# Modulation matrix-vector products of a transformer kernel: from TensorE to VectorE, GpSimd and ScalarE

## What is computed

```python
s_c = jax.nn.silu(c)
s_cc = jax.nn.silu(c_ctx)
for i in range(DEPTH):                                  # 2 layers
    mx = jnp.split((s_c @ ada_w[i] + ada_b[i])[:, None, :], N_MOD, axis=-1)
    mc = jnp.split((s_cc @ ada_w[i] + ada_b[i])[None, None, :], N_MOD, axis=-1)
    x = ffn_step(x, norm_g[i, 0], mx[0], mx[1], mx[2], ffn_w_in[i, 0], ffn_w_out[i, 0])
    xc = ffn_step(xc, norm_g[i, 0], mc[0], mc[1], mc[2], ffn_w_in[i, 0], ffn_w_out[i, 0])
...
def ffn_step(s, g, shift, scale, gate, w_in, w_out):
    return s + 0.5 * gate * swiglu(modulate(rms_norm(s, g), shift, scale), w_in, w_out)
```

## Time and profile before

| What | Value |
|---|---|
| median of 3 runs | 3329.41 us (3328.68 to 3330.70) |
| profiled execution: span from the first to the last instruction | 3327.2 us |
| PE busy, share of the span | 3144.5 us, 95% |
| DVE busy | 1994.1 us, 60% |
| ACT busy | 1111.8 us, 33% |
| POOL busy | 34.6 us, 1% |
| mean granted TensorE clock | 0.976 |

### The profile page before, as it was taken

How to read it: one execution, slowest core, us unless ns; L and a number is a source line. 1 busy time by engine, 2 the same in 40 slices (tenths; PEclk the granted TensorE clock), 3 DMA queues, 4 the chain that set the end, 5 groups by cost and what they waited for, 6 DMA issues and landing times.

```text
span 3327.2 us, 48292 instructions
## 1 busy us (share of the span) xinstructions
PE 3144.5 (95%) x19226; PEld 2638.7 (79%) x19226; DVE 1994.1 (60%) x2728; ACT 1111.8 (33%) x1124; POOL 34.6 (1%) x34
## 2 busy tenths in 40 slices
PE   6999997999999999998899899989989989998898
PEld 4777774777777888785699899847869979985798
DVE  6566567566665454546566666745656666664466
ACT  5333333333333222322343434321014334342333
POOL 0000002000000000000000000000000000000000
PEclk9999998999999999999999999989999999998999
DMA  7344440344441322131144354410014554432154
GB/s 307 128 165 163 174 152 13 139 151 164 164 165 63 113 76 108 69 132 46 39 173 179 124 189 176 145 38 1 1 43 164 189 171 163 178 139 45 64 189 164
DMA packets 59429, 421.56 MB, mean 127 GB/s; under 512 B 6600, under 2 KB 7752, under 8 KB 9392
## 3 DMA queue, kind: packets, MB, share of 16 engines
q1 hardware_dynamic: 57056, 407.33, 33.1%
q0 software_dynamic: 2288, 13.01, 1.7%
HBM read 419.24 MB, written 1.07 MB: 126 GB/s over the span
## 4 chain that ended last, share of the span: by engine, by line
PE 87%; DVE 8%; ACT 2%; issue 2%; DMA 1%; DVEq 0%; SPq 0%; ACTq 0%
PE ps_o L1466 9%; PE ps_o L1467 9%; PE ps_o L1468 9%; PE ps_g L1466 7%; PE ps_u L1467 7%; PE ps_g L1467 7%; PE ps_u L1466 7%; PE ps_u L1468 7%; PE ps_g L1468 7%; PE ps_g L1481 2%; PE ps_o L1473 2%; PE ps_o L1604 2%; PE ps_o L1605 2%; DVE wlo L840 2%; PE ps_o L1667 1%
## 5 line engine op out<-in xcount | busy, mean ns | idle before, releaser
L840 DVE TENSOR_TENSOR wlo<-wraw,whi 128x2048 fp32r<-128x2048 f32 x386 | 877.5, 2288 | 354.1 <-ACT whi L562 353.3
L562 ACT ACTIVATE whi<-wraw 128x2048 fp32r<-128x2048 f32 x386 | 733.3, 1911 | 1041.1 <-PE ps_u L1468 420.4
L1466 PE MATMUL ps_o<-ah,wlo 128*128 128x256 f32 (+1 forms) x1408 | 468.5, 333 | 15.2 <-issue 13.6
L1466 PE MATMUL ps_g<-hh,wlo 128*128 128x256 f32 (+1 forms) x1408 | 459.0, 326 | 17.7 <-DVE hl L865 12.2
L1467 PE MATMUL ps_o<-al,whi 128*128 128x256 f32 (+1 forms) x1408 | 459.1, 326 | 0.0
L1467 PE MATMUL ps_u<-hl,whi 128*128 128x256 f32 (+1 forms) x1408 | 458.6, 326 | 0.0
L1467 PE MATMUL ps_g<-hl,whi 128*128 128x256 f32 (+1 forms) x1408 | 458.2, 325 | 0.0
L1468 PE MATMUL ps_o<-ah,whi 128*128 128x256 f32 (+1 forms) x1408 | 457.5, 325 | 0.0
L1468 PE MATMUL ps_u<-hh,whi 128*128 128x256 f32 (+1 forms) x1408 | 456.9, 325 | 0.0
L1466 PE MATMUL ps_u<-hh,wlo 128*128 128x256 f32 (+1 forms) x1408 | 456.9, 325 | 0.0
L1468 PE MATMUL ps_g<-hh,whi 128*128 128x256 f32 (+1 forms) x1408 | 456.8, 324 | 0.0
(11 more groups left out here) (366 smaller groups left out, 3977.6 us busy)
## 6 DMA issues: line engine op xcount, KB each, us to landing
wraw<-in_W SPq DMA_DIRECT2D x387, 1024.0 KB, 4.8
scr<-bias_rows POOLq DMA_DIRECT2D x8, 384.0 KB, 8.1
x<-in_XT POOLq DMA_DIRECT2D x1, 2048.0 KB, 10.8
scr<-in_ICNT POOLq DMA_DIRECT2D x1, 2048.0 KB, 9.7
x<-in_MEMT POOLq DMA_DIRECT2D x2, 1024.0 KB, 7.8
cst<-in_CST POOLq DMA_DIRECT2D x1, 1799.5 KB, 15.1
out<-x SPq DMA_DIRECT2D x1, 1024.0 KB, 4.8
scr<-in_LORA POOLq DMA_DIRECT2D x1, 384.0 KB, 3.4
```

Of the source, the lines that this page charges most:

```text
L562: nc.scalar.activation(whi[:, n % SLOTS, :], wraw[:, n % SLOTS, :], ACT.Copy).then_inc(w_hi, 1)
L840: tt_(wlo[:, n % SLOTS, :], wraw[:, n % SLOTS, :], whi[:, n % SLOTS, :].bitcast(f32), sub).then_inc(w_lo, 1)
L1466: mm(out, a[1], b[0], start=first, stop=False)
```

## The change

ada_w no longer goes through `W` and PE. It is stored transposed as `ADA`, 144 blocks of 128 output features by 1024 (0.5 MB each). c and c_ctx come spread over all partitions (`CB`, 1 MB). For each block b, DVE multiplies it by silu(c) and sums along the row in one instruction (`ada_sum` on DVE); POOL multiplies it by silu(c_ctx) (`ada_products`) into one of two buffers, and ACT sums that one with an accumulating copy (`ada_sum` on ACT). Blocks lie in six slots of their own: SP issues the first 16 (shift and scale of FFN 0), POOL the rest, each after its slot has been read by both. 24 blocks come before the loop of FFN 0 (8 gate blocks of them between the norm and the loop), six in each of the 20 passes. The first norm goes tile by tile: tile d waits for the sums of blocks 2d and 2d + 1 only. `ada_turn`, the zeroing of rows and the 72 chunks of ada in the stream are gone. The table `icnt` of the pooling stage is a quarter of its size, and the constants of 1.8 MB (`cst` from `cos` on) are loaded after the last block, since the DVE sums write their unused product there.

```diff
-STREAM = [("ada", 0, [1] * ADA_FIRST), ("ffn", 0, FFN_ADA_TILES), ("pool", 0, [8]), ("ffn", 1, FFN_ADA_TILES),
+STREAM = [("ffn", 0, FFN_TILES), ("pool", 0, [8]), ("ffn", 1, FFN_TILES),
...
+            sp.dma_start(ada_c, CB).then_inc(cb_in, 16)
             sp.dma_start(vec[:], VEC).then_inc(c_in, 16)
-            for s in range(SLOTS):
+            for b in range(ADA_SLOTS):
+                block(b)
+            sp.dma_start(cst[:, 0:cat["cos"]], CST[:, 0:cat["cos"]]).then_inc(c_in, 16)
+            for s in range(2):
                 sp.dma_start(wraw[:, s, :], W[s * 128:(s + 1) * 128, :]).then_inc(w_here[s], 16)
...
+            for b in range(ADA_SLOTS, ADA_SCALE):
+                sp.wait_ge(ad_prod, b - ADA_SLOTS + 1)
+                sp.wait_ge(ad_dve, b - ADA_SLOTS + 1)
+                block(b)
...
+                for b in range(first, last):
+                    ada_landed(pool, b)
+                    if b >= 2:
+                        pool.wait_ge(ad_acc, b - 1)
+                    nc.gpsimd.tensor_tensor(ada_p[:, b % 2, :], ada_w[:, b % ADA_SLOTS, :], ada_c[:, 1, :], mult).then_inc(ad_prod, 1)
+                    if ADA_SCALE <= b + ADA_SLOTS < end:
+                        pool.wait_ge(ad_prod, b + 1)
+                        pool.wait_ge(ad_dve, b + 1)
+                        block(b + ADA_SLOTS)
...
+            def ada_sum(b, i=None):
+
+                act.wait_ge(ad_prod, b + 1 if i is None else i * ADA_PER_PASS + (b + 1))
+                p = ada_p[:, b % 2, :]
+                nc.scalar.activation(p, p, ACT.Copy, accum_out=mod_col(b, 1, i)).then_inc(ad_acc, 1)
...
                 for d in range(KT):
+                    if part == 0:
+                        if d == 2:
+                            split_hi(0)
+                            split_hi(1)
+                        if d:
+                            ada_sum(2 * d)
+                            ada_sum(2 * d + 1)
+                        act.wait_ge(ad_col, d + 1)
...
+                if f == 0:
+                    for b in range(ADA_SCALE, ADA_GATE):
+                        ada_sum(b)
                 silu(DONE[n0], g0 or None)
...
                     split_hi(n0 + 5, i, step, per)
+                    ada_sums(0, 2, i)
                     silu(i * step + DONE[n0 + 2], i + (g0 + 1))
+                    ada_sums(2, 4, i)
                     for n in range(n0 + 6, n0 + 5 + per):
                         if n - SLOTS == n_down:
+                            ada_sums(4, 6, i)
                             act.wait_ge(mm_done, i * step + DONE[n_down])
...
+                    if ada is not None:
+                        for b in range(ada, ada + ADA_PER_PASS):
+                            ada_sum(b, i)
+                    product(i + (g0 + 1), i * step + DONE[n_up])
+                    down(n_down, i * step + DONE[n_down - 1])
+                    hidden(i + (g0 + 1))
+                    split_lo(n_up + SLOTS, i, per)
+                    split_lo(n_down + SLOTS, i, per)
...
+            def ada_sum(b, i=None):
+
+                slot = b % ADA_SLOTS
+                ada_landed(dve, b, i)
+                if b >= 2:
+                    dve.wait_ge(ad_dve, b - 1 if i is None else i * ADA_PER_PASS + (b - 1))
+                stt(ada_junk[:, b % 2, :], ada_w[:, slot, :], 1.0, ada_c[:, 0, :], mult, mult, accum_out=mod_col(b, 0, i)).then_inc(ad_dve, 1)
```

More of the change, by code:

```diff
@@ L198, in pack @@
     for kind, i, _ in STREAM:
[L199 to L202, removed]
+        if kind == "ffn":
+            chunks += ffn_order(*(f1 + f2)[i])
         elif kind == "pool":
@@ L247, in ffn_pass @@
     def ffn_pass(f):
-        tiles = FFN_ADA_PASS if f < 2 else FFN_PASS
         n0 = FIRST["ffn", f]
[L251 to L254, removed]
+        n = len(FFN_PASS)
+        return n, sum(max(t, 1) for t in FFN_PASS), sum(FFN_PASS), n0 + 3, n0 + 4, n0 + 2 + n * (GROUPS - 1)
     with ExitStack() as ctx:
@@ L623, in hidden, with ada_sums @@
                     nc.scalar.activation(ah[:, :, 0:N], tmp[:, :, 0:N], ACT.Copy).then_inc(a_hi, 1)
-                per, step, _, _, n_down, _, n_last = ffn_pass(f)
+                per, step, _, _, n_down, n_last = ffn_pass(f)
+                ada = ADA_GATE + f * ADA_LOOP if f < 2 else None
+                def ada_sums(first, last, i):
+                    if ada is not None:
+                        for b in range(ada + first, ada + last):
+                            ada_sum(b, i)
+                if f == 0:
+                    for b in range(ADA_SCALE, ADA_GATE):
+                        ada_sum(b)
                 silu(DONE[n0], g0 or None)
@@ L908, in hidden, with down @@
                     tt_(al[:, :, 0:N], tmp[:, :, 0:N], ah[:, :, 0:N].bitcast(f32), sub).then_inc(a_ready, 1)
-                def down(n, done, between=lambda d: None):
+                def down(n, done):
                     for d in range(KT):
@@ L913, in down @@
                         residual(ps_o[:, (TILE0[n] + d) % BANKS, :], d, N, gate)
-                        between(d)
+                if f == 0:
+                    for b in range(ADA_SCALE, ADA_GATE):
+                        ada_sum(b)
+                    ada_gate()
                 product(g0, DONE[n0 + 1], g0 > 0)
@@ L1484, in sum_squares, with norm @@
                 st["sums"] = max(st["sums"], end)
-            def norm(N, split=True, part=None, again=False):
+            def norm(N, split=True, again=False):
                 if again:
@@ L1490, in norm @@
                 sum_squares(N, KT)
-                if part is not None:
-                    ada_turn(part)
-                keep_clock(N // 64 - 1 if part is None else 3, BANK[3])
+                keep_clock(N // 64 - 1, BANK[3])
                 st["k"], st["sums"] = st["k"] + 1, 0
@@ L1685, in y_split @@
                 pe.wait_ge(y_ready, st["y"])
-            pe.wait_ge(ad_lo, 1)
-            for n in range(ADA_FIRST):
-                ada(n)
-                sum_squares(NTOK, min(n - 2, KT))
-            norm(NTOK, part=0)
+            pe.wait_ge(c_in, 32)
+            norm(NTOK)
             ffn(0, NTOK)
-            norm(NTOK, False, part=1)
+            norm(NTOK, False)
             n = FIRST["pool", 0]
@@ L1706, in _ @@
             ffn(1, NTOK)
-            norm(NTOK, part=2)
+            norm(NTOK)
             ffn(2, NTOK)
```

242 lines of the change are left out of this document (109 added, 133 removed), and 1 row of the table sizes.

## The result

The changed kernel takes **3409.6 us** (median of 4 runs, 3406.9 to 3411.2) against 3329.1 us before on the same chip: **ratio 1.0237, 95% interval 1.0225 to 1.025**. It is slower by 80 us; 3388 was forecast, inside a range of 3285 to 3420.

The account below looks back on a forecast made before the run. PE was taken to bound the kernel, with new waits replacing the matmuls removed: +24 us in 20 passes, +38 ahead of the loop, -3 for the rest, so 3329.4 + 59 = 3388 us; range 3285 to 3420.

Parts of the forecast that it names:

- Price of the sum: One DVE sum of 1024 with accumulator: 1.35 us, about 1.1 of it holding the SBUF inputs.
- The third rival: DVE's sum takes two passes, 2.3 us, holding the inputs 2.2; 46.6 us a pass, 3532 us in all; chance 0.12.
- Price of the product and the turns: POOL's product: 2.2 us during which DVE's two-operand SBUF instructions stand still, plus 0.16 us for POOL to start.
- One pass: Loop pass: four of six sums behind products, 5.5 us PE gap in down projection; 40.4 us, +24 us over 20 passes.
- the clock: PE after the down projection's gap: granted clock falls to about half, costing 1.3 us a pass.
- The first rival: DVE keeps the SBUF inputs from one instruction to the next: pass 35.6 us, 3292 us in all; chance 0.20.
- No turns at all: DVE's accumulating sums never take turns with POOL: passes of 33.6 us, 3229 us in all; chance 0.12.
- Ahead of the loop: Start of the kernel: reciprocal done at 33.5, then 95 us of turns; loop starts at 130 us, 38 later.
- The lower bound of that step: Start without any turns: POOL products and DMA issues only, loop at 93 us, 1 us later than before.
- The rest: Outside the loops and start: `ada_turn` leaves three norms, -3 us (bounds -8 and 0); late constants and `icnt` nothing.

Follow-up runs that it names:

- e2: Changed kernel with DVE's sum reading one SBUF tensor, its product with silu(c) left out, POOL's product kept: 3262.7 us.
- e1: Changed kernel with POOL's product replaced by two fills that read nothing, so the silu(c_ctx) products are left out: 3247.8 us.
- e7: Changed kernel with six matmuls on constants ahead of the fifth tile of each looped down projection of FFN 0 and 1: 3376.9 us.
- e3: Changed kernel with the last two of each pass's six sums moved behind the eight residuals, everything computed: 3282.4 us, ratio to before 0.986.
- e10: e3 with the eight gate blocks' sums on ACT and DVE put behind the first SiLU, product and hidden split: 3282.6 us.
- e4: Changed kernel with both vectors' sums on DVE; POOL only issues block loads and ACT makes no sums: 3338.1 us.

## Why the prediction was right

Direction and mechanism in the loop held, and the time was 22 us too low. In the profiled executions it is 20: 11 in the loops and 9 at the start. By its own steps:

- **Price of the sum.** Forecast 1.35 us with 1.1 held; measured 1.22, 1.15 from start to start, the accumulator's read-out 0.08 us and beside the next sum. The third rival (two passes, 2.3 us) is ruled out, and with it, for this form, the rule of the Trainium skill, Vector Engine (DVE) Microarchitecture Reference, Points that are easy to get wrong: two f32 sources from SBUF with an accumulator, 1.15 us apart, ran as fast here as e2's sums with one source, 1.14 apart.
- **Price of the product and the turns.** Forecast 2.2 and 0.16; measured 2.40 with a sum waiting, 2.35 alone. The reading of rows 6 and 7 held to 0.1 us, also that operands in PSUM are not held. The Trainium skill, SBUF — State Buffer, Who interferes with whom, states that a VectorE instruction with two SBUF inputs contends with a GpSimd one that reads SBUF, not with one that only writes, and that the one issued second waits for the whole of the other. The trace agrees (3.42 us for 1.1 + 2.3), and so do e1 and e2.
- **One pass.** With time 0 at the gate's start (181.3), sums end at 31.5 (forecast 31.4), the first residual at 33.4 (33.5), the gap is 5.4 (5.5). The step that failed by its size is the clock: 1.3 us forecast, 1.9 measured by e7. The clock stood at 0.50 for 6.8 us of nearly every pass, 3.5 to 5.7 of them behind the gap, not for the 3 of the earlier trace rows. Most passes took 41.0 to 41.7 us instead of 40.4: the two loops cost 34.8 us with their junctions instead of 24.
- **The first rival** (DVE keeps the inputs) doesn't hold as a mechanism: the third sum waited in nearly every pass. But its condition, fewer than three products among the sums, came true once, in the window at 926 us: POOL idled 2.07 us ahead of its third product, and the last two sums of the pass, below, ran alone; the gap was 1.3 us, the clock stayed 1.00 and the pass 35. Why POOL idled stays open: the profile names ACT's sum, but the one that this product needs had ended at 934.5, 4 us before. That the pass stands so near this edge is what e3 used. *No turns at all* was forecast at 33.6 a pass, which e1 and e2 gave.

```profile
934.29 3.50 DVE L1009 SCALAR_TENSOR_TENSOR cst<-scr 128x1024 f32<-128x1024 f32 x1
...
937.72 1.22 DVE L1009 SCALAR_TENSOR_TENSOR cst<-scr 128x1024 f32<-128x1024 f32 x1
...
938.87 1.21 DVE L1009 SCALAR_TENSOR_TENSOR cst<-scr 128x1024 f32<-128x1024 f32 x1
```

- **Ahead of the loop.** The reciprocal ended at 36.98, not 33.5: PE's sums of squares lasted until 32.9. (Before, by the earlier trace rows, it ended at 60.52 + 3.35 = 63.87; the forecast was thus 30 us earlier, where I wrote 27.) The loop started at 138.2, not 130. The size was near, in part by luck, since the parts are wrong. I had summed 95 us in which every sum, split and norm step takes its turn; by e1 the turns are worth 20 us there, and of the 20 DVE sums behind the reciprocal only 8 were held (3.35 to 3.62 us, 12 at 1.22). I had given no price to the two small instructions ahead of each tile's norm step, which cost 15 of these 20 us. And I had left out what POOL does between two products, the wait of 0.30 and the issue of 0.59, as hidden by DVE's turn, and the round POOL, ACT, DVE, for which the products wait. The lower bound of that step, 93 us (its terms add up to 91.5), left out all turns; e1, which has none, came to 116.8, so the bound lacked the round.
- **The rest.** Forecast -3; measured -2.2 behind FFN 2's first SiLU. That isn't told from nothing: this stretch took 2285.3 us before, 2283.1 after, and 2283.2 to 2290.5 in the eleven experiments.

## What to carry to other kernels

Before work goes to GpSimd, ask what VectorE reads meanwhile: a two-input f32 product of 1024 on GpSimd took 2.4 us in which VectorE's own two-input instructions stood still, so it took from VectorE twice what the sum itself costs there (1.15 us); here both sums on VectorE were cheaper than one beside GpSimd. Work that must go beside a pipeline belongs behind the instruction that frees the next bank: the same six sums cost 7.5 us a pass ahead of the first residual, and nothing where two of them stood behind the last. What a hold costs goes by what waits behind the held instruction, not by its size: at the start two instructions of 0.16 us cost more than twice what the held sums cost. And a wait removed at one place of a chain over several engines can come back at another (e10).

## What the runs showed of the hardware that was not expected

- VectorE's back-to-back sums never kept GpSimd's product out: in every pass, a product that became ready during a sum ran before the next sum, which ended 1.09 us behind it (202.87 after 201.78).
- Two sums with accumulator follow each other in 1.15 us though one shows 1.22; the read-out of 0.08 us costs nothing.
- VectorE's two-input instructions of 4 and 2 numbers a partition took up to 2.26 us behind a product instead of 0.16: they are held like the sums of 1024.
- With a gap of 5.4 us the granted clock was 0.50 for 6.8 us in all passes of this kind but one (3.4 there). It fell while TensorE still stood, 1.1 us before the gap's end in the first pass of FFN 0 and 2.7 in the ninth, and the passes went from 41.7 to 41.0 us. Around gaps of 3.4 us (e4) the half clock lasted 6.8 and 3.4 us in turns, and the passes alternated between 39.8 and 38.6 us; with that of 1.3 us there was none.
- A fill on GpSimd, which reads nothing, held none of VectorE's instructions (e1).
